# First layer's MLP as seven half-block products in place of eight, with weight block sums by accumulating DMA and modulation products on GpSimd

## The reference

```python
mod = jnp.split((sc @ ada_w[l] + ada_b[l])[:, None, :], 6, axis=-1)      # sc = silu(c), latent tokens
mod_c = jnp.split(scc @ ada_w[l] + ada_b[l], 6, axis=-1)                 # context tokens
h = modulate(rmsnorm(x, norm1_w[l]), mod[0], mod[1])
...                                      # four token mixers, gates, output projection
x = x + mod[2] * gated_merge([ya, yb, yg, yd], p[4], w_branch[l], w_o[l])
x = x + mod[5] * sqrelu_mlp(modulate(rmsnorm(x, norm2_w[l]), mod[3], mod[4]), mlp_w1[l], mlp_w2[l])
...
def sqrelu_mlp(h, w1, w2):               # w1: 1024 x 4096, w2: 4096 x 1024
    return jnp.square(jax.nn.relu(h @ w1)) @ w2
```

## Time and profile before

| | |
|---|---|
| median of 3 runs | 2881.57 us (2879.72 to 2885.18) |
| the profiled execution, first to last instruction | 2877.3 us, 4.3 us under that median |
| PE busy | 2776.8 us, 97% of the span |
| DVE, ACT, POOL busy | 1573.5 us (55%), 1299.9 us (45%), 169.4 us (6%) |
| MLP of the first layer, first to last job | 1128.6 to 1672.7 us |
| moved by DMA | 275.61 MB, mean 96 GB/s |

### The profile page before, as it was taken

How to read it: one execution, slowest core, us unless ns; L and a number is a source line. 1 busy time by engine, 2 the same in 40 slices (tenths; PEclk the granted TensorE clock), 3 DMA queues, 4 the chain that set the end, 5 groups by cost and what they waited for, 6 DMA issues and landing times.

```text
span 2877.3 us, 37288 instructions
## 1 busy us (share of the span) xinstructions
PE 2776.8 (97%) x14792; PEld 2281.4 (79%) x14792; DVE 1573.5 (55%) x2382; ACT 1299.9 (45%) x2220; POOL 169.4 (6%) x196
## 2 busy tenths in 40 slices
PE   6999999999999999999999999999999999999998
PEld 4888886788887788888888878777677776788887
DVE  4568844456655467664444443884447544644434
ACT  4645434436645554553333344454546545433222
POOL 0023310000000000010000000230000000000000
PEclk9999999999999999999999999999999999999999
DMA  6322140031142052453333232234031311423232
GB/s 245 112 71 72 58 146 19 15 131 48 45 166 81 24 199 93 139 176 110 102 117 116 68 111 74 81 98 138 8 107 48 102 57 41 142 88 96 96 100 88
DMA packets 85453, 275.61 MB, mean 96 GB/s; under 512 B 9648, under 2 KB 9904, under 8 KB 84528
## 3 DMA queue, kind: packets, MB, share of 16 engines
q1 hardware_dynamic: 74896, 229.84, 23.8%
q0 software_dynamic: 10400, 43.59, 4.6%
HBM read 247.17 MB, written 26.22 MB: 95 GB/s over the span
## 4 chain that ended last, share of the span: by engine, by line
PE 82%; DVE 8%; ACT 4%; issue 3%; DMA 3%; SPq 1%; DVEq 0%; ACTq 0%; POOLq 0%
PE slot L736 79%; PE slot L1237 3%; DVE wl L1899 1%; DMA raw<-w_merge_dram 1%; ACT wh L1345 1%; ACT ada_prod L1798 1%; DVE ada_prod L2412 1%; DMA ada_first<-ada_dram 1%; DVE XS L2287 0%; DVE state L2266 0%; DVE XS L2229 0%; ACT SS L1745 0%; DVE SS L2241 0%; DMA x_kept<-X 0%; DMA raw<-w_dram 0%
## 5 line engine op out<-in xcount | busy, mean ns | idle before, releaser
L736 PE MATMUL slot<-Hh,wh 128*128 128x512 f32 (+1 forms) x2384 | 870.2, 366 | 21.5 <-DVE wl L1899 7.4
L736 PE MATMUL slot<-Hh,wl 128*128 128x512 f32 (+1 forms) x2384 | 834.3, 351 | 0.0
L736 PE MATMUL slot<-Hl,wh 128*128 128x512 f32 (+1 forms) x2384 | 833.9, 351 | 0.0
L1899 DVE TENSOR_TENSOR wl<-raw,wh 128x1024 fp32r<-128x1024 f32 (+1 forms) x332 | 379.5, 1143 | 271.7 <-ACT wh L1345 269.0
L736 PEld LDWEIGHTS slot<-Hh,wh 128*128 128x128 f32 x2384 | 451.9, 190 | 87.9 <-issue 17.5
L736 PEld LDWEIGHTS slot<-Hh,wl 128*128 128x128 f32 x2384 | 451.3, 190 | 60.7
L736 PEld LDWEIGHTS slot<-Hl,wh 128*128 128x128 f32 x2384 | 452.7, 190 | 57.3 <-issue 6.0
L1345 ACT ACTIVATE wh<-raw 128x1024 fp32r<-128x1024 f32 (+1 forms) x332 | 322.9, 973 | 383.2 <-PE slot L736 309.7
L736 PE MATMUL slot<-Uh,wh 128*128 128x512 f32 (+1 forms) x776 | 274.2, 353 | 2.5 <-DVE Ul L2467 1.3
L736 PE MATMUL slot<-Ul,wh 128*128 128x512 f32 (+1 forms) x776 | 273.4, 352 | 0.0
L736 PE MATMUL slot<-Uh,wl 128*128 128x512 f32 (+1 forms) x776 | 273.0, 352 | 0.0
(11 more groups left out here) (254 smaller groups left out, 3981.3 us busy)
## 6 DMA issues: line engine op xcount, KB each, us to landing
raw<-w_dram SPq DMA_DIRECT2D x204, 512.0 KB, 3.5
raw<-w_gate_dram SPq DMA_DIRECT2D x64, 512.0 KB, 3.5
ada_g_raw<-ada_dram POOLq DMA_DIRECT2D x48, 512.0 KB, 3.8
ada_g_raw<-ada_dram SPq DMA_DIRECT2D x32, 512.0 KB, 4.4
raw<-w_merge_dram SPq DMA_DIRECT2D x64, 256.0 KB, 3.0
g_kept<-logits_out SPq DMA_DIRECT2D x32, 384.0 KB, 2.3
SS<-g_kept SPq DMA_DIRECT2D x32, 384.0 KB, 4.2
ada_first<-ada_dram SPq DMA_DIRECT2D x8, 1024.0 KB, 17.8
```

The lines of the kernel that those rows point to most:

```text
L736: return pe.matmul(dst, lhsT, rhs, start=start, stop=stop)
L1899: dve.tensor_tensor(wl[to][:, 0:size, :], raw[p][:, 0:size, :], wh[to][:, 0:size, :].bitcast(f32), ALU.subtract).then_inc(low_done.sem, 1)
```

## The change

The MLP's products of the first layer are written as 2x2 block products with seven multiplications in place of eight (Winograd's form of Strassen's method). Features in and out are halved (4 tiles each, `HK`), and the 768 columns are halved too (384, `HT`). It is done for seven of the eight matrix products (`BLOCK_PHASES`: the first hidden half, `first`; then back and hidden halves in turn, `back`, `hidden`). The last back half stays as it was, with 8 jobs of 768 columns.

- **PE** (`block_mlp`): each phase has 7 products, each in two jobs (`h` = 0, 1) of two output tiles. A block job takes a whole weight tile's bytes (2 output tiles by 4 k-tiles) against 384 columns: 24 matmuls. 98 block jobs take the place of 56 jobs. Products 2, 3 and 4 (`ONTO`) accumulate on a slot that still holds an earlier product.
- **Weights**: the products need sums of weight blocks (`S1` to `S4`). POOL makes them in DRAM with plain copies and accumulating DMA (`weight_sums`, 8 transfers of 1 MB for each phase), two phases in branch A, three in B, two in D (`WEIGHT_SUMS`). SP waits for them before it loads.
- **Activations**: `HR` and `UR` hold the unsplit operands. For each product ACT makes a high part of 4x384 columns (`step_high`) and DVE the low part (`step_low`). DVE makes four operand sums in each back phase and in the first one (`operand_sum`), reads and combines the products (`read`, `add_gated`, `add_d`). The squares move from DVE to ACT (`squared_hidden`).
- **Modulation**: the last 7 products of the first layer and the 48 of the second move from DVE to POOL (`modulation_tiles`). ACT sums them at the block jobs of the table `ADA_AT`: 7 at jobs 3 to 12, 16 at every second job from 15 to 45, 32 at two jobs in three from 47 to 93.
- The loops over the two middle groups are gone in the first layer, where all is written out. The second layer's MLP stays a loop.

```diff
+HT, HK = T // 2, KT // 2
+BLOCK_ORDER = {"first": (1, 2, 5, 6, 3, 7, 4), "hidden": (1, 6, 2, 7, 5, 4, 3), "back": (1, 2, 5, 7, 3, 4, 6)}
...
+        ADA_EARLY, ADA_ALL = len(ADA_JOBS), N_GATE + ADA_TILES
+        ADA_AT = {i: ADA_EARLY + n for n, i in enumerate((3, 5, 6, 8, 9, 11, 12))}
+        ADA_AT |= {15 + 2 * n: N_GATE + n for n in range(ADA_BOTH)}
+        ADA_AT |= {47 + 3 * n // 2: N_GATE + ADA_BOTH + n for n in range(ADA_TILES - ADA_BOTH)}
...
+            def modulation_tiles():
+
+                pool.wait_ge(cs_back.sem, 16 * 3)
+
+                def load(t):
+                    pool.wait_ge(ada_read.sem, ADA_FIRST + t - 1)
+                    pool.dma_start(ada_raw[t % 2][:, :, :], w_ada[ADA_FIRST + t]).then_inc(ada_full[t % 2].sem, 16)
+
+                load(ADA_EARLY)
+                for t in range(ADA_EARLY, ADA_ALL):
+                    if t + 1 < ADA_ALL:
+                        load(t + 1)
+                    n, full = ada_sides(t), ada_full[t % 2]
+                    pool.wait_ge(full.sem, w.next(full))
+                    pool.wait_ge(ada_summed.sem, t - 1)
+                    tile = ada_raw[t % 2][:, :, :].rearrange("p k n -> p (k n)").unsqueeze(1).to_broadcast([P, n, D_MODEL])
+                    pool.tensor_tensor(ada_prod[t % 2][:, 0:n, :], cs_rows[:, 0:n, :], tile, ALU.mult).then_inc(ada_read.sem, 1)
+
+            def weight_sums(phase):
...
+                pool.dma_start(s1, a22).then_inc(sums_copied.sem, 16)
+                pool.dma_start(s3, a11).then_inc(sums_copied.sem, 16)
+                pool.dma_start(s2, a22).then_inc(sums_copied.sem, 16)
+                pool.dma_start(s4, a12).then_inc(sums_copied.sem, 16)
+                pool.wait_ge(sums_copied.sem, w.next(sums_copied, 4))
+                pool.dma_start(s3, a21, accum_op=ALU.add, max_dma_last_dim=4096).then_inc(sums_added.sem, 16)
+                pool.dma_start(s1, a21, accum_op=ALU.add, max_dma_last_dim=4096).then_inc(sums_added.sem, 16)
+                pool.wait_ge(sums_added.sem, w.next(sums_added, 2))
+                pool.dma_start(s2, s3, accum_op=ALU.add, max_dma_last_dim=4096).then_inc(sums_added.sem, 16)
+                pool.wait_ge(sums_added.sem, w.next(sums_added))
+                pool.dma_start(s4, s2, accum_op=ALU.add, max_dma_last_dim=4096).then_inc(sums_added.sem, 16)
+                pool.wait_ge(sums_added.sem, w.next(sums_added))
...
+                    if layer == 0:
+                        for phase in WEIGHT_SUMS[b]:
+                            weight_sums(phase)
                     pool.wait_ge(y_low.sem, w.next(y_low, outputs(b, layer)))
...
+                def part(where, w_high, w_low, x_high, x_low, k, fresh):
+                    for q in range(2):
+                        for a, (wp, xp) in enumerate(((w_high, x_high), (w_high, x_low), (w_low, x_high))):
+                            last = pe.matmul(slot[where][:, q * SEQ:q * SEQ + HT], wp[:, HK * q + k, :], xp[:, k, :],
+                                             start=fresh and k == 0 and a == 0, stop=k == HK - 1 and a == 2, skip_group_check=True)
+                    return last
...
+                def step_low(step):
+                    _, kind, _, _, product, _ = BLOCK_JOBS[2 * step]
+                    dve.wait_ge(block_high.sem, w.next(block_high))
+                    dve.tensor_tensor(B_LOW[step % 2][:, :, :], operand(kind, product), B_HIGH[step % 2][:, :, :].bitcast(f32),
+                                      ALU.subtract).then_inc(block_low.sem, 1)
...
+                for i, (phase, kind, s, h, product, where) in enumerate(BLOCK_JOBS):
+                    j = i - 14 * phase
...
+                        dve.wait_ge(job_done.sem, w.next(job_done))
+                        read(i - 1)
...
+                    if h == 0 and 2 <= i < N_BLOCK - 2:
+                        step_low(i // 2 + 1)
+                    if i:
+                        low(n_job + i + 2)
...
+                    if kind == "back" and j in (1, 2, 3, 5):
+                        if j == 1:
+                            dve.wait_ge(u_square.sem, squares_before(phase, 4))
+                        operand_sum({1: 1, 2: 2, 3: 3, 5: 4}[j], kind, phase)
```

562 lines of the change are left out of this document (442 added, 120 removed).

## The result

The changed kernel takes **2965.1 us** (median of 4 runs, 2958.5 to 2967.6) against 2882.4 us for the kernel before (4 runs beside it, 2879.7 to 2885.2): a ratio of **1.028, 95% interval 1.027 to 1.030**, slower by 83 us. The forecast was 2880.5 us, range 2845 to 2905. The profiled execution spans 2956.6 us, 79.3 more than before.

The account below looks back on a forecast made before the run. PE, 97% busy, was taken to bound the kernel. PE work -64 us, DVE lateness from POOL's lock +60, norm +3, weight sums 0 gave -1: a 2876 us profile, 2880.5 us as median, range 2845 to 2905.

Parts of the forecast that it names:

- The likeliest case: Whole kernel: terms sum to -1 us, so no measurable change (within 6 us) was called the likeliest result.
- The weight sums ... I take 0, with 0 to 10 us: Branches ahead of the MLP: 56 transfers of 1 MB contend with weight loads at a cost of 0, bounds 0 to 10 us.
- signs of being wrong: Changed profile: DVE's means unchanged, PE waiting for ACT or a weight transfer, or branch D beginning later than 819 us.
- After that all of its excess is PE's: MLP: DVE may be one job late; beyond that its lateness becomes PE waiting, 60 us over the phases.
- With 7 us at the ends 480: MLP: PE needs 406.9 us for block jobs, 66.4 for old jobs, 7 at the ends: 480, saving 64 us.
- PE's price: MLP: a matmul of 384 columns takes 173 ns, bounds 160 and 226; 24 make a block job of 4.15 us.
- rival 4: MLP: 384-column matmuls cost 226 ns, PE needs 125 us more, about 2945 us; chance 0.07 together with rival 3.
- The lock: MLP: DVE instructions with both inputs in SBUF stand still while POOL multiplies, less what is covered; 60 us of PE waits.
- what was to be seen: MLP profile: weight low part about 2 us in phases 0 to 2; PE waits 15 to 20 us in first two phases.
- The norm: Ahead of the MLP: POOL's first two products beside the norm delay DVE's work there, +3 us.
- Rival 2: MLP and norm: no product is covered and the engines' waits add up, 2911 us; chance 0.10.
- rival 3: Branches: accumulating transfers are slow, making POOL late for branch D's table and SP for sums, 2950 us; 0.07 with rival 4.

Follow-up runs that it names:

- e4: Changed kernel without weight sums (original blocks loaded instead) and with POOL's products cut to 16 of their 1024 columns: 2839.9 us, ratio 0.984 to the kernel before.
- e1: Changed kernel without its weight sums, original weight blocks of the same size loaded in their place: 2924.0 us, ratio 1.014 to the kernel before.
- e3: Changed kernel without weight sums and with the MLP's modulation products on DVE instead of POOL: 2876.5 us, ratio 0.997 to the kernel before.
- e12: Changed kernel without weight sums, each POOL product made in pieces of 512 columns: 2893.6 us, ratio 1.003 to the kernel before.

## Why the prediction was wrong

The likeliest case was no change, and the measured time lies 60 us above the range. Two steps failed: the weight sums were put at 0 and cost 41 us, and a wait of PE was priced at its length alone, without the slower clock behind it, 31 us. A third term, the idle time near the turns of phases, was missing with 12 us. The sum of the steps was -1 us and the span grew by 79.3, so 80.3 us are to be found. Step by step:

- **"The weight sums ... I take 0, with 0 to 10 us": failed, 41 us.** The bounds were made from shares and volumes (DMA busy 21%, 76 us of room per phase, which took 46 to 58 in place of the estimated 29) and said rightly that POOL would be in time. Two of the prediction's own signs of being wrong stood in the changed profile, a load that PE waits for (through ACT and DVE), and branch D's table later than 819 us. What decides is how long one small load takes beside transfers of 1 MB of which four, then two, are issued at once, the four in pieces ten times its own; and the merge stage, where jobs are shortest, is where the sums begin. The rows had the landing time of one load but no transfer beside it, and the step took the absence of a row for the absence of a cost. The upper bound from the rows was there: the four copies at the 3.6 us per MB of the earlier trace rows are 14.5 us, and a load issued behind them could land that late, in each of the phases begun while merges run.
- **"After that all of its excess is PE's": failed by half, 31 us short.** The steps turned a late DVE into as much lost PE time and left the clock out. In the changed kernel PE's 2743 matmuls take 510.4 us where at full clock they would be some 479 (98 x 4.15 + 66.4, and the norms' 6). The MLP before doesn't show it, since its longest wait is 1.5 us.
- **"With 7 us at the ends 480": 19 us short, 12 of them new.** e4, with nothing to lock, has 498.7 us: 6.6 of it the clock, counted above, and 12.8 us idle (1.5 and 1.9 us in the first phase, 3.2 in the second, 4.2 for the hidden low parts ahead of the last eight jobs, 1.5 at layer 1's norm). These are dependencies near the turn of a phase that a sum of durations doesn't see. The last term of 12 us is the difference of idle time: 73.0 us against 60 and 1 of the 7 at the ends.
- **PE's price was right:** 173 ns, 24 to a job; rival 4 is out.
- **The lock was right in kind, and nearly in size by chance.** Forecast 60 us of PE waits; measured 60.2 beyond those of e4 (73.0 less 12.8), and 56.7 in e1. But the way there was not: the sum gave DVE some 145 us of lost time (175 of products less 31 covered), and it lost 106 us (463.6 less e4's 357.5), while PE paid more for each microsecond. e3 shows why: DVE loses nearly as much (83 us) to its own products and PE pays less than half as much. That a single instruction of 6 us is beyond PE's lead of one job, and short ones are not, fits this but is argued: e12 did not part length from amount. Of what was to be seen, the low part's mean in phases 0 to 2 (1.89 us) came as forecast, and so did PE's waits: 16 and 18 us in the first two phases, none in phase 4.
- **The norm:** 3 us forecast; a wait of 3.3 us is there (e1 and the changed kernel), and the start of the MLP in e1 is 3.6 us later, within what starts differ.
- **The rivals.** Rival 2 (products uncovered) had the MLP at 568 us by more lost DVE time than there was; rival 3's 2950 us is the nearest number, but by a late POOL, which never was late. No rival held a load that is late beside the sums' transfers, or the clock.

Together: 41 + 31 + 12 = 84 us, less the 3.7 us of layer 1, are the 80.3.

What stays open: how much of the lock's cost is its length and how much its amount (e12 moved both), how the sums' cost divides between copies and accumulating transfers, and what in layer 1, whose matmuls no kernel changed, differs by up to 10 us between profiles (1200 to 1210 us).

## What to carry to other kernels

Before work is moved from DVE to GpSimd, compare what DVE itself would take: 2.29 us on DVE against 4.58 us of a lock that reaches past a job of 4.15 us made the move a loss of 47 us, although DVE had time left on average. A bulk transfer off the critical path is not judged by DMA's busy share but by what a 0.5 MB load sees beside it: issue such transfers one at a time (33 us of 42 won back here), or the copies in pieces about as small as the loads' (28). And a wait of PE cost up to one and a half times its length here, where the clock fell after it.
